# Expert rows dealt to trunk stages by a table, and summed on VectorE where the trunk uses TensorE

## The reference

```python
def block(xb):                                   # 128 tokens
    q = (xb @ w_q).reshape(PEER_BLOCK, PEER_HEADS, 2, PEER_QDIM // 2)
    ...                                          # top 16 of 256 candidates for each of 8 heads
    e_idx = jnp.take_along_axis(cand_idx, pos, axis=-1)
    gate = jax.nn.softmax(top_s, axis=-1)
    u_sel = u[e_idx]
    v_sel = v[e_idx]
    act = jax.nn.gelu(jnp.einsum('thkd,td->thk', u_sel, xb).astype(f32), approximate=False)
    return jnp.einsum('thk,thkd->td', (gate * act).astype(xb.dtype), v_sel)
```

## Time and profile before

| | |
|---|---|
| median of three runs | 4819.0 us |
| the profiled execution | 4816.17 us |
| its span | 4814.4 us |
| granted TensorE clock, mean | 0.891 |
| busy, share of the span | PE 77%, PEld 48%, DVE 60%, ACT 37%, POOL 29% |
| instructions | 49161 |
| moved from HBM | 1309.61 MB, 272 GB/s over the span |
| laps, by the first dot of each | lap 0 to 670 us, lap 1 to 1801, lap 2 to 2957, lap 3 to 4094, tail to 4814 |

### The profile page before, as it was taken

One profiled execution on the slowest core, in us unless ns is written; L12 is line 12 of the kernel. 1 busy time (PEld: TensorE's weight loads), 2 busy tenths in 40 slices (PEclk: granted clock), 3 DMA queues, 4 the chain that ended last, 5 costly groups with the idle time before them and its releaser, 6 DMA issues.

```text
span 4814.4 us, 49161 instructions
## 1 busy us (share of the span) xinstructions
PE 3703.2 (77%) x14204; PEld 2330.4 (48%) x14204; DVE 2887.6 (60%) x6043; ACT 1802.0 (37%) x4482; POOL 1392.2 (29%) x1140
## 2 busy tenths in 40 slices
PE   7898957779788956776889884777978885477576
PEld 5677743456465633334656562335646563122222
DVE  2322268676576477756645548866657746964644
ACT  2222224422455423433255632442255633233333
POOL 0100012343222222233322222233322222246564
PEclk8899979989899978898899996998989997799898
DMA  7113347856787879895578877785677787799997
GB/s 255 66 55 107 114 174 290 340 194 217 284 299 279 330 284 359 303 408 210 190 280 312 320 275 268 291 339 196 224 281 299 290 323 271 280 362 417 404 413 322
DMA packets 247821, 1314.92 MB, mean 273 GB/s; under 512 B 21248, under 2 KB 35456, under 8 KB 116480
## 3 DMA queue, kind: packets, MB, share of 16 engines
q0 software_dynamic: 147456, 1073.81, 58.9%
q1 hardware_dynamic: 100096, 237.98, 13.7%
HBM read 1309.61 MB, written 2.10 MB: 272 GB/s over the span
## 4 chain that ended last, share of the span: by engine, by line
DVE 24%; PE 23%; issue 11%; PEld 11%; ACT 9%; DMA 7%; DVEq 6%; POOL 4%; ACTq 2%; PEldq 2%; SPq 0%; POOLq 0%
DVE row L1480 9%; PE bank L591 7%; DMA row<-uv,e_idx 5%; PEld bank L638 4%; POOL row L1862 4%; PE bank L652 3%; PE bank L759 3%; DVEq L1481 2%; PEld bank L652 2%; DVE reg L1368 2%; PE bank L970 2%; PEld bank L902 2%; DVE e_acc L1449 2%; PE bank L750 1%; DVE reg L1363 1%
## 5 line engine op out<-in xcount | busy, mean ns | idle before, releaser
L1862 POOL DMA_INDIRECT row<-uv,e_idx x1024 | 1248.6, 1219 | 3089.2 <-PE bank L591 1744.2
L591 PE MATMUL bank<-row,e_diag 128*128 128x512 f32 x2884 | 1536.4, 664 | 634.7 <-ACT e_diag L1046 550.7
L1480 DVE CUSTOM_DVE_ANT_0 row<-row,e_h 128x1024 f32<-128x1024 f32 x1024 | 1291.2, 1261 | 537.0 <-DMA row<-uv,e_idx 373.5
L591 PEld LDWEIGHTS bank<-row,e_diag 128*128 128x128 f32 x2884 | 552.3, 206 | 1396.7 <-ACT e_diag L1046 695.1
L1039 ACT ACTIVATE e_ge<-e_dot 128x1 f32<-128x1 f32 x1024 | 207.2, 202 | 1671.8 <-DVEq L1481 1658.0
L652 PE MATMUL bank<-hT,weights 128*128 128x256 f32 (+2 forms) x2176 | 516.4, 392 | 24.6 <-DMA weights<-w_in 16.8
L652 PEld LDWEIGHTS bank<-hT,weights 128*128 128x128 f32 (+2 forms) x2176 | 414.4, 192 | 156.2 <-issue 67.5
L1449 DVE SCALAR_TENSOR_TENSOR e_acc<-row,e_wg,e_acc 128x1024 f32<-128x1024 f32 x295 | 392.2, 1329 | 146.1 <-ACTq L1043 113.9
L638 PE MATMUL bank<-hT,weights 128*128 128x256 f32 x1536 | 352.9, 383 | 23.1 <-issue 18.7
L638 PEld LDWEIGHTS bank<-hT,weights 128*128 128x128 f32 x1536 | 285.3, 190 | 94.2 <-issue 53.3
L1041 ACT ACTIVATE e_wg<-e_gate,e_ge 128x1 f32<-128x1 f32 x1024 | 301.5, 294 | 74.0 <-issue 3.2
(11 more groups left out here) (252 smaller groups left out, 3717.8 us busy)
## 6 DMA issues: line engine op xcount, KB each, us to landing
weights<-w_ada SPq DMA_DIRECT2D x48, 1024.0 KB, 9.1
weights<-w_mac SPq DMA_DIRECT2D x64, 768.0 KB, 6.0
weights<-w_in SPq DMA_DIRECT2D x44, 1024.0 KB, 8.5
weights<-w_mb SPq DMA_DIRECT2D x32, 768.0 KB, 7.1
weights<-w_out SPq DMA_DIRECT2D x16, 1024.0 KB, 8.6
weights<-w_pq SPq DMA_DIRECT2D x16, 1024.0 KB, 8.8
row<-uv,e_idx POOLq DMA_INDIRECT x1024, 7.9
weights<-w_in SPq DMA_DIRECT2D x8, 1056.0 KB, 8.8
```

What stands on the lines that cost most here:

```text
L591: last = mm(acc_ps[k][:, :], e_diag[:, r, :], row[r][:, D + k * NB:D + (k + 1) * NB], start=(e, j) in PE_FIRST, stop=(e, j) in PE_LAST)
L1480: V.tensor_tensor_reduce(row[r][:, 0:D], row[r][:, 0:D], e_h[t][:], 1.0, 0.0, ALU.mult, ALU.add, e_dot[:, r:r + 1])
L1862: pool.indirect_dma_start(row[r], None, uv, bass.IndirectOffsetOnAxis(ap=e_idx[:, j:j + 1], axis=0)).then_inc(rows_landed[r], 16)
```

## The change

1. `Plan` no longer multiplies costs by a pace. It notes where each phase begins, and `done()` maps the plan's time on to slot numbers: a phase takes as many slots as PACE names for it and for this half. `Turns` then counts in slots.
2. `on_dve` no longer starts at slot 70 with two of five. Beside the first 8 and last 4 slots of a tile, it puts two of three slots of the scan on VectorE and every slot from gla to the end of out; none in prep, pq and route. The tail keeps its 24.
3. A dot signals `dots` itself, without a drain and without the `passed` increment; a drain now stands ahead of each sum on VectorE.
4. Second halves of weight blocks are placed at the middle between a step's opening and full time.

```diff
-PACE = dict(head=2.0, prep=4.0, scan=1.35, gla=1.0, dsa=1.0, mac=1.0, att=1.5, mb=1.0, out=1.0, pq=1.0)
+PACE = dict(head=(8, 6), prep=(74, 76), scan=(47, 47), gla=(22, 22), dsa=(8, 9), mac=(24, 18), att=(4, 6), mb=(21, 21), out=(8, 8),
+            pq=(12, 14), route=(30, 31))
...
+        def clock(x):
+            name, a, b, at_ = [ph for ph in self.phases if ph[1] <= x][-1]
+            return at_ + PACE[name][self.h] * (x - a) / (b - a)
+
+        self.open_at = {n: clock(x) for n, (x, _y) in self.from_to.items()}
+        self.full_at = {n: clock(y) for n, (_x, y) in self.from_to.items()}
...
-DVE_FROM = 70
...
 def on_dve(e, j):
     s = j % SLOTS
     if s < HEAD_DVE or s >= SLOTS - TAIL_DVE:
         return True
-    return e < LAPS - 1 and j >= DVE_FROM and j % 5 in (1, 3)
+    if e == LAPS - 1:
+        return False
+    at = PLANS[e + 1].begins
+    if at["scan"] <= j < at["gla"]:
+        return j % 3 > 0
+    return at["gla"] <= j < at["pq"]
...
-    def __init__(self, steps=None, lag=0.0, plan=None):
+    def __init__(self, steps=None, lag=0.0):
         self.steps, self.i = steps, 0
-        self.pace = plan.total / (N_SLOT + 2) if plan else 0.0
-        self.lag = lag * self.pace
+        self.lag = lag
 
     def upto(self, at):
-        while self.steps is not None and self.i * self.pace + self.lag <= at:
+        while self.steps is not None and self.i + self.lag <= at:
             self.step()
...
-                                turns.upto(plan.full_at[name] - COST / 2)
+                                turns.upto(plan.open_at[name] / 2 + plan.full_at[name] / 2)
...
                     dve.wait_ge(wg_ready, DVE_COUNT[n])
+                    dve.drain()
...
                     dve.wait_ge(rows_landed[r], 16 * (n // RING + 1))
-                    dve.sem_inc(passed, 1)
-                    V.tensor_tensor_reduce(row[r][:, 0:D], row[r][:, 0:D], e_h[t][:], 1.0, 0.0, ALU.mult, ALU.add, e_dot[:, r:r + 1])
-                    dve.drain().then_inc(dots, 1)
+                    V.tensor_tensor_reduce(row[r][:, 0:D], row[r][:, 0:D], e_h[t][:], 1.0, 0.0, ALU.mult, ALU.add, e_dot[:, r:r + 1]).then_inc(dots, 1)
```

More of the change, by code:

```diff
@@ L95, with __init__, phase, close @@
 class Plan:
-    def __init__(self):
-        self.order, self.open_at, self.full_at, self.now, self.pace = [], {}, {}, 0.0, 1.0
+    def __init__(self, h):
+        self.h, self.order, self.phases, self.from_to = h, [], [], {}
+        self.now = 0.0
+    def phase(self, name):
+        self.close()
+        self.phases.append([name, self.now, self.now, self.now])
+    def close(self):
+        if self.phases:
+            self.phases[-1][2] = self.now
     def one(self, name, cost):
         self.order.append(name)
-        self.open_at[name] = self.now
-        self.now += cost * self.pace
-        self.full_at[name] = self.now
+        self.from_to[name] = self.now, self.now + cost
+        self.now += cost
     def group(self, names, cost):
-        half = cost * self.pace / 2
+        half = cost / 2
         for i, name in enumerate(names):
             self.order.append(name)
-            self.open_at[name] = self.now + i * half
-            self.full_at[name] = self.now + (len(names) + i + 1) * half
+            self.from_to[name] = self.now + i * half, self.now + (len(names) + i + 1) * half
         self.now += 2 * half * len(names)
-PACE = dict(head=2.0, prep=4.0, scan=1.35, gla=1.0, dsa=1.0, mac=1.0, att=1.5, mb=1.0, out=1.0, pq=1.0)
+    def done(self):
+        self.close()
+        self.begins, at = {}, 0.0
+        for ph in self.phases:
+            self.begins[ph[0]] = at
+            ph[3] = at
+            at += PACE[ph[0]][self.h]
+        self.total = at
+        def clock(x):
[3 more added lines that the diff above has]
+        self.full_at = {n: clock(y) for n, (_x, y) in self.from_to.items()}
+        self.routing = [clock(x) for x in self.routing]
+        return self
+PACE = dict(head=(8, 6), prep=(74, 76), scan=(47, 47), gla=(22, 22), dsa=(8, 9), mac=(24, 18), att=(4, 6), mb=(21, 21), out=(8, 8),
+            pq=(12, 14), route=(30, 31))
 COST = 3.5
-ROUTE_US, ROUTE_PIECES = 9.0, 8
+ROUTE_PIECES = 8
 def lap_plan(h):
-    p = Plan()
+    p = Plan(h)
     def ada(g, *mods):
@@ L129, in ada @@
                 p.one(("mod", m), 0.5)
-    p.pace = PACE["head"]
+    p.phase("head")
     p.one(("ss", 0), COST)
@@ L134, in lap_plan @@
         ada(g, *mods)
-    p.pace = PACE["prep"]
+    p.phase("prep")
     p.one(("rp", 12), COST)
@@ L154, in lap_plan @@
             p.one((n, c), 0.5)
-    p.pace = PACE["scan"]
+    p.phase("scan")
     for half, t, q, stage in rwkv_steps():
@@ L168, in lap_plan @@
             p.one(n, 0.8)
-    p.pace = PACE["gla"]
+    p.phase("gla")
     for c in range(4):
@@ L221, in lap_plan @@
         p.one(("br", m, 1), COST / 2)
-    p.pace = PACE["out"]
+    p.phase("out")
     p.group([("wo", m) for m in range(4)], COST)
@@ L236, in lap_plan @@
             p.one(("sc", t, k, q), 1.0)
-    p.routing = p.now
-    p.now += ROUTE_US * ROUTE_PIECES
-    p.total = p.now
+    p.phase("route")
+    p.routing = [p.now + i for i in range(ROUTE_PIECES)]
+    p.now += ROUTE_PIECES
     for x in range(2):
-        p.one(("h2", 1, x), 0.5)
-    return p
+        p.one(("h2", 1, x), 0.1)
+    return p.done()
 def lap_rows(h):
@@ L1325, in _ @@
                     scores(t, q)
-                turns.upto(plan.routing + 6 * ROUTE_US)
+                turns.upto(plan.routing[6])
                 soft(lap, 0, 0)
@@ L1507, in _ @@
                 modc = modc_all[:, 48 * l:48 * l + 48]
-                turns = Turns(expert_steps(lap - 1), 0.0, plan) if lap else Turns()
+                turns = Turns(expert_steps(lap - 1)) if lap else Turns()
                 def cl(name, i=0, n=1):
@@ L1831, in _ @@
                 for i in range(ROUTE_PIECES):
-                    turns.upto(plan.routing + i * ROUTE_US)
+                    turns.upto(plan.routing[i])
                     piece(i, lap, 0, 0)
```

20 lines of the change are left out of this document (10 added, 10 removed).

## The result

The changed kernel takes 4667.5 us, the median of four runs (4656.5 to 4682.7), against 4819.0 before (4815.5 to 4825.7). The ratio is 0.968 (95% interval 0.966 to 0.970). The profiled run was the longest of the four: 4682.7 us, span 4680.9. So its parts add up to 133 us less than before, where the medians show 151.

The account below looks back on a forecast made before the run. C was taken as bound by TensorE, A of lap 2 by transfers, A of lap 1 nearest by VectorE. Laps 1 and 3 at -50 each and lap 2 at -58 gave -158, so 4661 us (range 4590 to 4735).

Parts of the forecast that it names:

- C, laps 1 and 3: Gla to out, second and fourth laps (a lap: one half-sequence of one layer): 65 us less each as rows leave TensorE.
- C, lap 2: Gla to out in the third lap: 34 us less, with 87 slots for 91 and all rows on VectorE.
- B: The scan: 16 us more a lap, with 47 slots and a VectorE row priced dearer than a TensorE row.
- A, lap 2: Head and prep of the third lap, bound by transfers: 44 us less as 98 slots become 82.
- A, laps 1 and 3: Head and prep, VectorE nearest to full: 8 us less each; idle time at dots goes, five slots are added.
- D: Pq and routing, transfers late: 7 us more in laps 1 and 3, 4 in lap 2; routing slots at 2.8 us.
- The dots: Dots on VectorE without drain: 0.27 us idle saved each; A 16 us, B 4, D 5 per lap; 75 in all.
- The tail: The last 256 slots alone, 720 us at 0.92 of the DMA engines: no change from a new dealing.
- C at its floor: Rival: gla to out falls to its floor and the scan does not grow: 4541 to 4590 us; chance 0.15.
- The drain is worth nothing: Rival: the idle 0.27 us ahead of a dot stays, the sum loses 75 us: 4736 us; chance 0.12.
- TensorE's clock: Rival: without rows in C TensorE's granted clock falls, 50 us a lap, 4811 us, no change; chance 0.06.
- VectorE stuck on ScalarE: Rival: VectorE rows in C wait for ScalarE's weights; 0.64 us more a row cancels the gain; chance 0.12.

Follow-up runs that it names:

- K1: Kernel before with the edit at the dots alone (dots signal themselves, drain ahead of a sum on VectorE), old planner: 4742.9 us, ratio 0.984.
- K4: Changed kernel with nearly the old table (the phases get the slots of the kernel before) in the new planner: 4611.6 us, ratio 0.958.
- K3: Changed kernel with the old rows rule (from slot 70 on two of every five on VectorE): 4742.1 us, ratio 0.985.
- K5: K4 with the scan's rows of laps 1 and 3, and most of lap 2's, on TensorE: 4670.5 us, ratio 0.969.
- K2: Changed kernel with the dots as before (drain and extra semaphore step at each dot, none ahead of a sum): 4768.6 us, ratio 0.989.
- K8: K4 with five row buffers instead of six: 4720.3 us (two runs), ratio 0.979; tail 754 us.
- K10: Changed kernel with the drain behind each dot again, none ahead of a sum, without the separate step of `passed`: 4715.4 us, ratio 0.978.
- K11: K4 with A's rows by the old rule (slots 70 and above, two of five, on VectorE): 4634.7 us, ratio 0.962.
- K12: K4 with D's rows by the old rule (two of five on VectorE): 4634.2 us, ratio 0.961.

## Why the prediction came out, point by point

The forecast was 4661 us and the time is 4667.5. The way there holds in part; one term was credited to the wrong cause.

- **C, laps 1 and 3 (-65).** -66 and -59. More than half of it is not what I had said. From before over K1 and K4 to the changed kernel, C of lap 1 goes 488, 478, 459, 422 us: 11 for the dots, 18 for the rows (and the planner), 37 for the 20 slots that left. K3 against the changed kernel gives 28 and 24 us for the rows rule alone at 84 slots. I had counted on the rows for all of it, with seven tenths of the full gain of 93 us. That the two numbers met is luck.
- **C, lap 2 (-34).** -54. Here the rows rule is worth 42 us alone (K3) and 54 with the planner (K1 to K4). The mechanism held, and the seven tenths were too low.
- **B (+16).** +21, +13 and +21, close, but for the wrong reason. I had a VectorE row at 2.28 us and a TensorE row at 1.24; K5 shows the TensorE row dearer by 0.4 us in lap 1. Five more slots above the point at 42 cost 25 us there (K4 to the changed kernel). The two unknowns came out of two windows with nearly the same slots, so their difference took up whatever else differed.
- **A, lap 2 (-44).** -47, and by the mechanism given: the transfers' share stayed at 0.93 while 16 slots left. But the slots had to go elsewhere, and B and D of the same lap charged 43 us for them.
- **A, laps 1 and 3 (-8).** 0 and +3 (lap 3's A is 293 us before). The dots saved 12 us (K2), the five slots took them back. This is within the ends that I gave, -14 and +15.
- **D (+7, +4).** +13, +14 and +20. The step that failed is the price of a routing slot by the tail's 2.8 us: route takes 93, 95 and 108 us in laps 1, 2 and 3 where that price gave 87, 84 and 87. The slots of pq came near their price: 60, 55 and 64 us against 60, 56 and 60. Waits of VectorE in D of lap 1, before and after:

```profile
DVE row L1480 <- DMA row<-uv,e_idx: 8.3, 5, 2.9
```

```profile
DVE row L1512 <- DMA row<-uv,e_idx: 57.4, 23, 6.0
```

The transfers are late there as foreseen, at a share of only 0.83. The waits on ScalarE went, 26.8 us against 1.4 after.

- **The dots (75 us in the sum).** 74 alone, 101 with the rest, and 16 of it in the tail, where I had put nothing: my argument was that at a share of 0.92 only the transfers count. K1's tail (705 us) and K8 refute it.
- **The tail (0).** -16, see K8 and K1.

**The rivals.** *C at its floor* did not come: 4541 to 4590 lies below even K4. *The drain is worth nothing* fell with K1, K2 and K10. The Trainium skill (VectorE: DVE Perf Modes, "The DRAIN you can't avoid") says that chaining without semaphores skips no flush and that the semaphore costs nothing extra. That is about the flush behind every operation and a semaphore on each copy, and I had stretched it to an explicit drain and a step of its own, of which it says nothing. These do cost: the dots are 1.51, 1.40 and 1.15 us apart with step and drain, with the drain, and with neither. At 1.15 us no gap shows for the signal that rides on the dot. The same section adds that a next operation that is not held starts earlier, and the dots agree, the second starting 0.08 us before the first has ended. *TensorE's clock* did fall in C, from 0.92 and 0.94 to 0.87 and 0.90, and in K4 to 0.85 and 0.87, and K4 is the faster one. The trunk's own matmuls in C of lap 1 were busy 316 us before, 324 after and 341 in K4. So the rival was real in kind, but it cost 8 us of busy time in the lap where it had 50. *VectorE stuck on ScalarE*: the waits of VectorE in C of lap 1 after the change have this row, against 13.3 us for 49 rows:

```profile
DVE e_acc L1482 <- ACTq L1075: 5.7, 3, 3.7
```

That is 0.07 us for each of 84 rows, where 0.64 was needed for a loss.

**What stayed hidden.** My sum went part by part and never asked what the table is worth by itself. It took the slots that leave C and A of lap 2 as gains, and priced those that arrive in B, D and A by means. Measured by itself the table loses 56 us with the new rows; with the old ones, table and planner together give nothing. The forecast was still close by luck, because the errors cancel: laps 1 and 3 gave 32 and 15 us instead of 50 each, while lap 2 gave 74 instead of 58 and the tail 16 instead of none; that makes 137, less 4 us by which lap 0 grew, and the medians add the 18 us between the 133 of the profiled runs and 151.

**Open.** Whether a rows rule by phase shortens C of laps 1 and 3 in K4 (459 us with 104 or with 73 rows on VectorE), why C grew in K5, and why the old rules of K11 and K12 cost some 20 us away from their own part. The table alone and the rows rule alone, with the old dots, were not run, nor the planner or item 4 of the change by itself, nor the semaphore step without a drain.
